# Neighbourhood biases read backwards by VectorE instead of turned by products on TensorE

## The reference

```python
GRID_W, NA_MAX_KH, NA_KW = 64, 8, 16      # 256 tokens are 4 rows of 64
kh = min(NA_MAX_KH, rows)                 # 4
dc = np.clip(kc[:, None, :] - c[:, :, None] + NA_KW - 1, 0, 2 * NA_KW - 2)
...
dr = rs + jnp.arange(kh) - r + NA_MAX_KH - 1
bias = rpb[:, dr][:, :, dc].transpose(0, 2, 3, 1, 4)
s = jnp.where(mask_j, s + bias.astype(jnp.float32), NEG_INF)
```

## Time and profile before

| | us |
|---|---|
| median of 3 runs | 1364.94 |
| lowest and highest of them | 1363.85, 1365.16 |
| profiled execution | 1364.45 |
| its span | 1362.6 |
| TensorE busy (products) | 1308.6 (96%) |
| VectorE busy | 912.6 (67%) |
| ScalarE busy | 700.2 (51%) |
| GpSimd busy | 142.4 (10%) |
| mean granted clock of TensorE | 0.977 of full speed |

### The profile page before, as it was taken

The page is one execution under the profiler, slowest core; times in us unless marked ns, Lnnn a source line. Parts: engine busy times, 40 slices in busy tenths (PEclk is TensorE's granted clock), DMA queues, the critical chain, the costliest instruction groups (busy, mean ns, idle before and its releaser), DMA issues.

```text
span 1362.6 us, 19889 instructions
## 1 busy us (share of the span) xinstructions
PE 1308.6 (96%) x8210; PEld 1168.9 (86%) x8210; DVE 912.6 (67%) x1065; ACT 700.2 (51%) x908; POOL 142.4 (10%) x166
## 2 busy tenths in 40 slices
PE   8999999999899999999898999999999999899997
PEld 7889888888698888898788888879999988888886
DVE  6766655566946655566777665587888775766666
ACT  5445545455645444543654444446877763354442
POOL 0000000004505000000000000000144543000000
PEclk9999999999699999999899999998999999999999
DMA  9555666645139666554124555535444424465551
GB/s 308 189 182 157 199 185 187 190 149 188 30 109 217 213 190 190 180 185 156 63 94 155 194 193 196 191 122 185 125 155 124 155 94 155 155 216 185 186 185 62
DMA packets 221034, 224.61 MB, mean 165 GB/s; under 512 B 7312, under 2 KB 204304, under 8 KB 220816
## 3 DMA queue, kind: packets, MB, share of 16 engines
q1 hardware_dynamic: 217760, 213.94, 49.1%
q10 hardware_dynamic: 2160, 7.31, 1.5%
q0 software_dynamic: 1024, 2.10, 0.9%
HBM read 222.27 MB, written 1.05 MB: 164 GB/s over the span
## 4 chain that ended last, share of the span: by engine, by line
PE 75%; DVE 14%; ACT 4%; issue 3%; DMA 2%; POOL 1%; SPq 0%; DVEq 0%; ACTq 0%
PE ps L480 19%; PE ps L681 17%; PE ps L494 11%; PE ps L482 10%; DVE wlo L1480 4%; PE ps L642 2%; PE ps L462 2%; PE ps L949 2%; ACT whi L1064 2%; PE ps L453 1%; PE ps L452 1%; PE ps L451 1%; DVE ssm_taps L1869 1%; DVE small L1691 1%; DMA raw<-in_ffn_w_gate_up 1%
## 5 line engine op out<-in xcount | busy, mean ns | idle before, releaser
L1480 DVE TENSOR_TENSOR wlo<-raw,whi 128x2048 fp32r<-128x2048 f32 x202 | 461.8, 2292 | 167.1 <-ACT whi L1064 166.9
L480 PE MATMUL ps<-act,whi 128*128 128x512 f32 x1280 | 454.0, 398 | 3.1 <-DVE act L1500 2.4
L1064 ACT ACTIVATE whi<-raw 128x2048 fp32r<-128x2048 f32 x202 | 384.6, 1907 | 55.5 <-PE ps L681 31.3
L482 PE MATMUL ps<-act,wlo 128*128 128x256 f32 x1280 | 359.3, 281 | 0.0
L480 PEld LDWEIGHTS ps<-act,whi 128*128 128x128 f32 x1280 | 240.5, 188 | 63.1 <-DVE wlo L1480 2.6
L482 PEld LDWEIGHTS ps<-act,wlo 128*128 128x128 f32 x1280 | 241.7, 189 | 1.6
L1111 ACT ACTIVATE low_sb<-ps 128x512 f32<-128x512 f32 x88 | 52.5, 596 | 200.3 <-PE ps L482 191.6
L494 PE MATMUL ps<-whi,act 128*128 128x256 f32 x736 | 136.4, 287 | 1.1 <-DVE act L1545 1.1
L494 PEld LDWEIGHTS ps<-whi,act 128*128 128x128 f32 x736 | 116.1, 194 | 2.7 <-DVE act L1545 1.3
L1597 DVE TENSOR_TENSOR sum_sb<-ps,low_sb 128x512 f32<-128x512 f32 x88 | 60.5, 687 | 81.6 <-ACT low_sb L1111 81.6
L681 PE MATMUL ps<-whi,hidhi 128*128 128x512 f32 x368 | 114.3, 392 | 0.0
(11 more groups left out here) (231 smaller groups left out, 2031.5 us busy)
## 6 DMA issues: line engine op xcount, KB each, us to landing
raw<-in_mlp_w SPq DMA_DIRECT2D x128, 512.0 KB, 4.4
raw<-in_ffn_w_gate_up SPq DMA_DIRECT2D x88, 512.0 KB, 5.1
raw<-in_ssm_w_in SPq DMA_DIRECT2D x50, 512.0 KB, 4.7
raw<-in_ffn_w_down SPq DMA_DIRECT2D x44, 512.0 KB, 4.8
raw<-in_conv_w_in SPq DMA_DIRECT2D x24, 512.0 KB, 5.8
raw<-in_attn_w_in SPq DMA_DIRECT2D x18, 512.0 KB, 4.7
raw<-in_ssm_w_out SPq DMA_DIRECT2D x16, 512.0 KB, 4.4
raw<-in_attn_w_qkv SPq DMA_DIRECT2D x12, 512.0 KB, 4.4
```

The source lines that it names most:

```text
L480: e.matmul(ps[:, b + f, :].rearrange("p (a n) -> p a n", a=2), hi[:, k, cols], act[:, :, k, :], start=k == 0, stop=False, skip_group_check ...
L482: last = e.matmul(ps[:, b + f, 0:T], lo[:, k, cols], act[:, 0, k, :], start=False, stop=k == KT - 1, skip_group_check=True)
L1064: e.activation(whi[s][:, :], raw[s][:, :], ACT.Copy).then_inc(*rounded.up(c))
L1480: e.tensor_tensor(wlo[s][:, :], raw[s][:, :], f32(whi[s][:, :]), ALU.subtract).then_inc(*split.up(c))
```

## The change

The table is stored in HBM with each row reversed. The same gathers then bring in tiles in which the queries stand in the right order and each run of 64 keys is reversed. VectorE reads them with a step of -1 inside each 64 keys and adds the mask in the same instruction; the products and the table `flip` are gone. A tile can't be written over itself when it is read in falling order, so every tile is written one place further: the gathers of tile n (n = 2m + g) land in the place of tile n - 1, those of tile 0 in a new place `rpb_spare`, which lies in the FFN's hidden buffer. Its 8 gathers therefore wait for FFN1's last product and are issued last. The additions run from the last tile to the first: tiles 3 and 2 after n = 3, tiles 1 and 0 after n = 5, each behind the one before.

```diff
+        rpb_spare, _ = place("rpb_spare", [P, 4, T], offset=hid_at + 8192)
...
+        def rpb_mirrored(m, g):
+            n = 2 * m + g
+            return rpb_tile((n - 1) // 2, (n - 1) % 2) if n else rpb_spare[:, :, :]
...
-            def flip_rpb(m):
-                if m == 0:
-                    e.wait_ge(rpb_landed, 16 * 32)
-                for g in range(2):
-                    if m:
-                        e.wait_ge(*flip_biased(m - 1, g))
-                    tile = rpb_tile(m, g).rearrange("p u n -> p (u n)")
-                    for n in range(2):
-                        last = e.matmul(ps[:, ACC + 2 * g + n, :], table[:, TAB["flip"]:TAB["flip"] + P],
-                                        tile[:, 512 * n:512 * n + 512], start=True, stop=True)
-                    last.then_inc(*flipped.up(m, g))
...
-                    if n in (3, 5):
-                        flip_rpb(n // 4)
...
-            def flip_rpb(m):
-                near = spread(table[:, TAB["near"] + m * T:], [0, 4], [1, T])
-                for g in range(2):
-                    e.wait_ge(*flipped(m, g))
-                    e.tensor_tensor(rpb_tile(m, g), ps[:, ACC + 2 * g:ACC + 2 * g + 2, :].rearrange("p a (b n) -> p (a b) n", b=2),
-                                    near, ALU.add).then_inc(*flip_biased.up(m, g))
+            def near_bias(m):
+                near = spread(table[:, TAB["near"] + m * T:], [0, 4], [64, 4], [1, 64])
+                if m == 1:
+                    e.wait_ge(rpb_landed, 16 * 32)
+                for g in (1, 0):
+                    if (m, g) != (1, 1):
+                        e.wait_ge(*near_biased(m if g == 0 else 1, 1 - g))
+                    mirrored = spread(rpb_mirrored(m, g)[:, 0, 63:], [T, 4], [64, 4], [-1, 64])
+                    e.tensor_tensor(rpb_tile(m, g).rearrange("p u (a n) -> p u a n", a=4), mirrored, near,
+                                    ALU.add).then_inc(*near_biased.up(m, g))
...
                     if n in (3, 5):
-                        flip_rpb(n // 4)
+                        near_bias(1 - n // 4)
...
-            for m in range(MT):
-                for head in range(8):
+            for n in (1, 2, 3, 0):
+                m, g = divmod(n, 2)
+                if n == 0:
+                    e.wait_ge(*multiplied(FFN1 + 32))
+                for head in range(4 * g, 4 * g + 4):
                     for rr in range(2):
                         src = bass.AP(rpb.tensor, head * sh + (7 - 2 * m - rr) * sr, [[1, 64], [sr, 4], [1, 64]])
-                        dst = rpb_tile(m, head // 4)[64 * rr:64 * rr + 64, HEADS.index(head % 4), :]
+                        dst = rpb_mirrored(m, g)[64 * rr:64 * rr + 64, HEADS.index(head % 4), :]
                         e.dma_start(dst.rearrange("p (a n) -> p a n", a=4), src).then_inc(rpb_landed, 16)
...
-    arrays["rpb"] = np.pad(rpb, ((0, 0), (0, 0), (48, 48)))
+    arrays["rpb"] = np.ascontiguousarray(np.pad(rpb, ((0, 0), (0, 0), (48, 48)))[:, :, ::-1])
```

More of the change, by code:

```diff
@@ L225, in build @@
         heads_turned, scored, probs_turned, mixed = (signal(n) for n in ("heads_turned", "scored", "probs_turned", "mixed"))
-        flipped, dt_turned, xs_turned, bordered = (signal(n) for n in ("flipped", "dt_turned", "xs_turned", "bordered"))
+        dt_turned, xs_turned, bordered = (signal(n) for n in ("dt_turned", "xs_turned", "bordered"))
         gram, cum_summed, crossed, inner, y_turned = (signal(n) for n in ("gram", "cum_summed", "crossed", "inner", "y_turned"))
@@ L243, in build @@
         biased, weigh_step, topped, normed, out_lo = (signal(n) for n in ("biased", "weigh_step", "topped", "normed", "out_lo"))
-        flip_biased, rope_step, roped, dt_step = (signal(n) for n in ("flip_biased", "rope_step", "roped", "dt_step"))
+        near_biased, rope_step, roped, dt_step = (signal(n) for n in ("near_biased", "rope_step", "roped", "dt_step"))
         ssm_tap, edge_scaled, parts_step, rows_made = (signal(n) for n in ("ssm_tap", "edge_scaled", "parts_step", "rows_made"))
@@ L2180, in spans @@
     return out, n
-TAB, TAB_N = spans([("ident", P), ("le", P), ("ge", P), ("gt", P), ("lt", P), ("flip", P), ("dist", 2 * T), ("window", 2 * T),
+TAB, TAB_N = spans([("ident", P), ("le", P), ("ge", P), ("gt", P), ("lt", P), ("dist", 2 * T), ("window", 2 * T),
                     ("near", 2 * T), ("cos", 2 * HD), ("sin", 2 * HD)])
@@ L2205, in shape_tables @@
     put("lt", a < b)
-    put("flip", a == b // 64 * 64 + 63 - b % 64)
     far = np.float32(1e30)
```

## The result

| | before | after |
|---|---|---|
| median (5 runs each) | 1365.16 | 1357.36 |
| lowest to highest | 1363.85 to 1366.65 | 1356.78 to 1359.34 |
| ratio, 95% interval | | 0.9944, 0.9932 to 0.9955 |
| profiled execution | 1364.45 | 1358.19 |
| its span | 1362.6 | 1356.4 |

The changed kernel is faster by 7.8 us by the medians; the forecast was 1357.0. The two profiled executions differ by only 6.2 us in their spans. The trace shows where the rest is.

The account below looks back on a forecast made before the run. The third layer's projection was taken as bound by TensorE's own work, end to end. Gains of 6.88 + 0.8 = 7.7 us gave 1356.8 from the profiled execution, 1357.2 from the median; forecast 1357.0 us, range 1355.3 to 1359.9.

Parts of the forecast that it names:

- First term: Third layer's projection: the 8 turning products leave TensorE's queue, two pieces of 3.44 us on the chain, gaining 6.88 us.
- next late things: Projection: VectorE's splits that TensorE needs next; all forecast in time, the tightest 3.1 us early, so cost 0.
- Additions: Projection: VectorE's four 128x1024 additions from SBUF, one input read falling, take 1.22 us each and cost 0 in the sum.
- The covers: Projection: how early VectorE's splits are done before TensorE needs them; additions delay nothing below 3.3 us each.
- t = 3.3: Projection: the time in us of one addition from which TensorE's chunk behind the first two additions would be late.
- the formula: Projection: if one addition takes t us, its last chunk is late by 4t - 13.5 us.
- Wait for the gathers: VectorE's wait ahead of the first addition, at 621.5 us: last gathers land at 607.3, 14 us ahead.
- Second term: FFN1's start: 8 gathers no longer run beside its weight loads, gaining 0.8 us, with bounds 0 and 1.1.
- The late load: A weight load at FFN1's start that ScalarE waits for: landing forecast to fall from 15.04 to some 13 us.
- Rival 1: Attention and all behind it come 7 us earlier, and lower clock gives some gain back: 1360.0 us, chance 8%.
- the tail: End of an attention, where TensorE is the chain: 3 us at half clock lose 1.5 us.
- Rivals 2 to 4: In projection: VectorE becomes the bound (1367.5 us, 4%); a wait fills the products' place (1359.8, 5%); loads hold chunks (1364.5, 3%).

## Why the prediction was right

*First term, 6.88 us.* Measured 6.86: 50.36 or 50.37 us in every kernel without the products, save the one with its additions five times over, against 57.21 or 57.22 in each with them. Taking them out alone gave it, putting idle ones back took it away. None of the next late things came up.

*Additions.* 1.22 us was taken, 1.22 to 1.23 measured. The rule of the Trainium skill that was weighed, in Vector Engine (DVE) Microarchitecture Reference, section 5.2 (full rate only on runs of adjacent words from an 8-byte boundary), would have slowed the additions only if a falling run counted as broken. The traces show that it does not: an addition takes 1215 to 1226 ns falling against 1217 to 1226 rising, 1.2 ns a column with its fixed part. This measures what its section 5.1 leaves open for a negative step, for this form. The covers held on both sides of t = 3.3, though not at it: nothing was lost at 2.5 us, and 12.9 at 6.3, where the formula gives 11.7.

*Wait for the gathers.* 14 us of room were forecast and 18 found, as a gather in an empty stretch lands after 2.8 us.

*Second term, 0.8 us.* Real, and right in size by the mean over the traces (1.0) with 0.5 in the first profile. The late load came down to 14.43 us, not to 13: a quarter less in the queue ahead of it freed 0.6 us of it, not the 2 that I had read from 3.0 us of engine time. What counted was ScalarE's wait for it, and half of that went in this trace, not all of it as I had taken for the 0.8. That the size still came out near the mean is in part luck.

*Rival 1.* Its mechanism showed in the profile (1.85 us in the second attention), but does not belong to the change: the second profile of before has it too, and one kernel without the products lacks it. The place was not the tail that the rival named. The chance of 8% was for a lasting loss, and there was none. What I had missed is how much a single profile can be off: the two of the kernel before differ by 3.0 us in span with an unchanged program (1.7 of it ahead of FFN0's norm, 1.8 in the second attention), while I put the scatter at 0.7 each way from three runs within 1.3 us. In the runs on all chips the kernel before ranged from 1360.0 to 1369.3. Two of the thirteen traces are also 2.6 us shorter behind the state-space mixer's norm (443.9 us against 446.4), with nothing changed there. So luck had a part in how close the total came: the two terms are shown, but 1357.0 against 1357.4 us is nearer than the scatter of single executions allows one to claim, and it was helped by the profile and the median of before lying within 0.5.

*Rivals 2 to 4.* VectorE did not become the bound, for an addition took 1.22 us and the loss begins beyond 2.5. No wait filled the products' place, and the loads kept up.

## What to carry to other kernels

Work that sits in the queue of the engine that is the chain is worth its full length, start to start, once each other engine's next deadline has been worked out and found met. A reversal that the vector engine did by its access pattern, in an instruction that it ran anyway, cost nothing here. Count the DMAs that a change moves, at the place they leave as well as where they go: here a quarter of 2.1 MB of gathers was worth 1 us, since they crowded weight loads that TensorE was waiting for. Before a difference in one stage of two profiles is explained, profile the unchanged kernel twice. And an instruction that is to fill an idle time has to stand in front of the wait that makes it: look in the trace where it landed.

## What the runs showed of the hardware

- VectorE reads a 128x1024 fp32 operand in falling order of each 64 words as fast as in rising order: 1215 to 1226 ns against 1217 to 1226.
- A gather of 64 KB issued by GpSimd landed after 2.8 us (median) in an empty stretch; among weight loads the medians are 5.3 us for the first 16 and 6.5 or 6.9 for those behind them. Its issue takes 0.63 us in the empty stretch and 0.63 to 0.73 among the loads.
- A TensorE wait of 3.8 us cost more than itself: behind it a chunk took 7.36 us instead of 5.94, at a granted clock of 0.58 over some 4 us. Behind a wait of 6.0 us the next two chunks took 1.4 us longer together.
- Forty products of a zero tile in TensorE's idle times held the clock at 1.00 from 650 to 670 us, in a stretch where VectorE is busy for 19.0 of 20 us, and won nothing. With more of them at two more places, the ones ahead of MLP0 behind the wait, the kernel took 4 us longer.
- The profiles of one unchanged kernel differed by 3.0 us in span, at mean granted clocks of 0.977 and 0.978.
